# Splitting the squares of queries and keys: two fp32r products in place of one fp32 product

## The reference

```
def rmsnorm(x, g):
    xf = x.astype(jnp.float32)
    y = xf * lax.rsqrt(jnp.mean(xf * xf, axis=-1, keepdims=True) + EPS)
    return (y * g.astype(jnp.float32)).astype(x.dtype)
```

## Time and profile before

| | us |
|---|---|
| median of 3 runs | 3531.56 |
| lowest and highest | 3531.51, 3531.73 |
| profiled execution, its own time | 3533.1 |
| span of the profile (first to last instruction) | 3531.3 |
| attention layers, in the span | about 2340 to 3531 |
| TensorE's mean granted clock over the span | 0.985 of full |

### The profile page before, as it was taken

One profiled execution on the slowest core, in us unless ns is written; L12 is line 12 of the kernel. 1 busy time (PEld: TensorE's weight loads), 2 busy tenths in 40 slices (PEclk: granted clock), 3 DMA queues, 4 the chain that ended last, 5 costly groups with the idle time before them and its releaser, 6 DMA issues.

```text
span 3531.3 us, 45519 instructions
## 1 busy us (share of the span) xinstructions
PE 3380.8 (96%) x16418; PEld 2772.2 (79%) x16418; DVE 1505.3 (43%) x2496; ACT 1325.5 (38%) x2112; POOL 1414.2 (40%) x1040
## 2 busy tenths in 40 slices
PE   8999998899999999999979999979999999998898
PEld 7888876788888888887768888867777777887677
DVE  2221455552215522136565221472575377335633
ACT  3222435442224422233554222463344244444343
POOL 5554433045545455443304554343432433452222
PEclk9999999999999999999999999989999999999999
DMA  4322211022222232221202222322211221231111
GB/s 153 98 98 96 84 66 54 7 96 95 95 96 96 81 98 95 90 95 66 66 1 84 95 95 96 106 84 84 72 66 48 84 66 60 78 125 60 42 54 60
DMA packets 76660, 281.30 MB, mean 80 GB/s; under 512 B 8512, under 2 KB 8640, under 8 KB 76128
## 3 DMA queue, kind: packets, MB, share of 16 engines
q1 hardware_dynamic: 75600, 274.66, 23.6%
q10 hardware_dynamic: 912, 4.59, 0.4%
HBM read 277.12 MB, written 2.10 MB: 79 GB/s over the span
## 4 chain that ended last, share of the span: by engine, by line
PE 87%; DVE 7%; ACT 3%; issue 2%; DMA 1%; DVEq 0%; ACTq 0%; SPq 0%
PE ps L1795 16%; PE ps L1797 16%; PE ps L1796 16%; PE ps L1867 4%; PE ps L1869 4%; PE ps L1868 4%; PE ps L2316 2%; PE ps L2330 2%; PE ps L1906 2%; PE ps L1904 2%; PE ps L1905 2%; PE ps L2377 2%; PE ps L2257 1%; PE ps L2259 1%; PE ps L2258 1%
## 5 line engine op out<-in xcount | busy, mean ns | idle before, releaser
L545 POOL TENSOR_TENSOR w_lo<-raw,w_hi 128x512 fp32r<-128x512 f32 x1028 | 1402.6, 1387 | 2093.6 <-ACT w_hi L596 2093.5
L1795 PE MATMUL ps<-x_hi,w_hi 128*128 128x512 f32 x2560 | 1045.3, 408 | 4.6 <-issue 4.6
L1797 PE MATMUL ps<-x_hi,w_lo 128*128 128x512 f32 x2560 | 999.2, 390 | 0.0
L1796 PE MATMUL ps<-x_lo,w_hi 128*128 128x512 f32 x2560 | 998.6, 390 | 0.0
L596 ACT ACTIVATE w_hi<-raw 128x1024 fp32r<-128x1024 f32 x514 | 542.2, 1057 | 1099.0 <-PE ps L1797 617.7
L1795 PEld LDWEIGHTS ps<-x_hi,w_hi 128*128 128x128 f32 x2560 | 481.8, 188 | 125.1 <-issue 29.0
L1796 PEld LDWEIGHTS ps<-x_lo,w_hi 128*128 128x128 f32 x2560 | 481.7, 188 | 117.8 <-issue 22.1
L1797 PEld LDWEIGHTS ps<-x_hi,w_lo 128*128 128x128 f32 x2560 | 481.2, 188 | 102.6
L1224 DVE TENSOR_TENSOR T<-T,ps 128x512 f32<-128x512 f32 x66 | 45.3, 687 | 497.0 <-PE ps L1797 490.8
L1904 PE MATMUL ps<-h_hi,w_hi 128*128 128x512 f32 (+1 forms) x440 | 153.2, 348 | 0.0
L1906 PE MATMUL ps<-h_hi,w_lo 128*128 128x512 f32 (+1 forms) x440 | 152.5, 347 | 0.0
(11 more groups left out here) (330 smaller groups left out, 5088.8 us busy)
## 6 DMA issues: line engine op xcount, KB each, us to landing
raw<-in_weights SPq DMA_DIRECT2D x514, 512.0 KB, 3.3
Y<-in_x_t SPq DMA_DIRECT2D x1, 2048.0 KB, 7.9
mem<-in_mem_t ACTq DMA_DIRECT2D x2, 1024.0 KB, 7.2
out_t<-Y SPq DMA_DIRECT2D x8, 256.0 KB, 2.2
ple_p<-in_p_t ACTq DMA_DIRECT2D x2, 512.0 KB, 5.1
mat<-in_mats SPq DMA_DIRECT2D x1, 768.0 KB, 11.7
masks<-in_masks ACTq DMA_DIRECT2D x1, 768.0 KB, 8.4
rope<-in_rope_b ACTq DMA_DIRECT2D x1, 512.0 KB, 8.1
```

The source lines that it names most:

```text
L545: ins = pool.tensor_tensor(g.wl[:, k, part], g.raw[:, k, part], g.wh[:, k, part], ALU.subtract)
L1795: mm(out, wh[:, c], xh[:, kc, :], start=kc == 0, stop=False)
L1796: mm(out, wh[:, c], xl[:, kc, :], start=False, stop=False)
L1797: ins = mm(out, wl[:, c], xh[:, kc, :], start=False, stop=kc == DC - 1)
```

## The change

`g.T` slots 0 and 1, which were two buffers of squares, become one square (slot 0) and its high part (slot 1), under the name `g.SQ` in fp32r. ScalarE squares into slot 0, waits for that, and copies it to slot 1, which rounds to fp32r. POOL subtracts slot 1 from slot 0 in place (`square_low`). TensorE multiplies both parts by ones in fp32r into the same sum. The three tiles of `FAST` (r = 7, 31 and 65), whose sums are not inside a unit, keep the fp32 product. The memory keys, 256 columns wide, use the two halves of a slot in turn. On POOL, `square_low` of a unit u stands behind the low part of unit u+3 and ahead of that of unit u+4. A `Sum` inside a unit is issued ahead of chunk 6 and no longer ahead of chunk 4; groups stay ahead of chunk 4 and now come first in `mid`.

```diff
+        g.SQ, _ = place("square_parts", (P, 2, S), F32R, squares)
+        g.ones, _ = place("ones_r", (P, P), F32R)
@@ between
-            out.append(op._replace(mid=tuple(held) + ((op.mid,) if op.mid else ())))
+            out.append(op._replace(mid=((op.mid,) if op.mid else ()) + tuple(held)))
+FAST = (R_MEM[0] + 7, R_A + 23, R_B + 1)
+def parts(r):
+    return r + 1 - sum(f <= r for f in FAST)
+def square_cols(r, width):
+    return slice(r % 2 * N_MEM, r % 2 * N_MEM + N_MEM) if width == N_MEM else slice(0, width)
@@ pool_program
+    def square_low(r, width):
+        cols = square_cols(r, width)
+        pool.wait_ge(s.sqhi_done, parts(r))
+        pool.tensor_tensor(g.SQ[:, 0, cols], g.T[:, 0, cols], g.SQ[:, 1, cols], ALU.subtract).then_inc(s.sqlo_done, 1)
+    for i in range(2):
+        for r in range(2):
+            low_many(at, BASE["AB"][i] + (8, 6)[i])
+            at = BASE["AB"][i] + (8, 6)[i]
+            square_low(R_MEM[i] + r, N_MEM)
+        for op in PLANS[i]:
+            if isinstance(op, Unit) and op.r is not None and op.r not in FAST:
+                low_many(at, op.u + 4)
+                at = op.u + 4
+                square_low(op.r, N_MEM if op.kind == "mem_k" else S)
@@ norm (ScalarE, once)
+            fn(g.ones[:, :], g.mat[:, M_ONES, :], ACT.Copy).then_inc(s.ones_done, 1)
@@ qk_square
+        cols = square_cols(r, width)
         act.wait_ge(s.qraw_done, r + 1)
-        if r >= 2:
+        if width == S or r % 56 < 2:
+            if r >= 2:
+                act.wait_ge(s.qss_mm, r - (r % 56 == 1))
+        else:
             act.wait_ge(s.qss_mm, r - 1)
-        fn(g.T[:, r % 2, 0:width], src, ACT.Square).then_inc(s.qsq_done, 1)
+        fn(g.T[:, 0, cols], src, ACT.Square).then_inc(s.qsq_done, 1)
+        if r not in FAST:
+            act.wait_ge(s.qsq_done, r + 1)
+            fn(g.SQ[:, 1, cols], g.T[:, 0, cols], ACT.Copy).then_inc(s.sqhi_done, 1)
@@ tile
-            if kc == DC // 2:
-                for op in mid:
+            for op in mid:
+                if kc == (DC // 2 if isinstance(op, Group) else DC - 2):
                     item(op)
@@ item of a Sum
-            pe.wait_ge(s.qsq_done, r + 1)
+            cols, out = square_cols(r, width), ps[:, 2, 0:width]
             if r:
                 pe.wait_ge(s.qrs_done, r)
-            mm(ps[:, 2, 0:width], ones, g.T[:, r % 2, 0:width], start=True, stop=True).then_inc(s.qss_mm, 1)
+            if r in FAST:
+                pe.wait_ge(s.qsq_done, r + 1)
+                mm(out, ones, g.T[:, 0, cols], start=True, stop=True).then_inc(s.qss_mm, 1)
+            else:
+                pe.wait_ge(s.ones_done, 1)
+                pe.wait_ge(s.sqlo_done, parts(r))
+                mm(out, g.ones[:, :], g.SQ[:, 1, cols], start=True, stop=False)
+                mm(out, g.ones[:, :], g.SQ[:, 0, cols], start=False, stop=True).then_inc(s.qss_mm, 1)
```

More of the change, by code:

```diff
@@ L137, in build @@
         g.XL, _ = place("x_lo", (P, DC, S), F32R)
-        g.T, _ = place("T", (P, 7, S), F32)
+        g.T, squares = place("T", (P, 7, S), F32)
+        g.SQ, _ = place("square_parts", (P, 2, S), F32R, squares)
         g.vec, _ = place("vec", (P, N_VEC), F32)
@@ L209, in build @@
             e_done qdec_done ks_done r_done vn_mm vn_done o_mm o_copied ds_mm s_done osq_done oss_mm osr_done
-            memhi_done memlo_done qraw_done qsq_done qss_mm qrs_done qk_done vcopy_done
+            memhi_done memlo_done qraw_done qsq_done sqhi_done sqlo_done ones_done qss_mm qrs_done qk_done vcopy_done
             s_mm smax_done p_done pn_done pt_mm ptc_done o_mm2 o_done gate_done silu_g_done gout_done ohi_done olo_done proj_copied
```

## The result

| | before | after |
|---|---|---|
| median (4 runs each) | 3531.61 us | 3551.88 us |
| lowest and highest | 3531.51, 3531.73 | 3551.55, 3557.17 |
| ratio to before | | 1.0057, interval 1.0045 to 1.0069 |
| span of the profiled execution | 3531.3 | 3550.1 |

The change makes the kernel slower by 20 us. I predicted 3521, in a range up to 3534: the direction is wrong, and the time lies above the range.

A forecast was written before the change was run, and what follows sets the result against it. TensorE was taken to bound most cycles and VectorE some; -9.0 + 1.2 - 1.1 + 1.2 + 1.0 - 5.1 + 1.0 = -10.8 us, giving a median of 3520.8, predicted as 3521, range 3507 to 3534 (forecast's own 3512 to 3527).

The forecast's parts named there:

- The gain of the products: TensorE's sums: two fp32r products save 0.40 us per wide sum, 0.2 per narrow one, 27 us at most.
- POOL goes in front of L1601 and again in front of L1602, 0.98 each: VectorE's rotation: POOL's third instruction brings two blocks, making the chain 0.78 us longer in each of 48 units.
- The fourth rival: VectorE's chain: each block lasts POOL's whole 1.26 us, chain 1.34 longer a unit, +11, 3543; chance 5%.
- The lead of L1600 over POOL is then only 0.1; I take off 0.6: Six heads with groups: each gains 2.1 us, cut to 1.5 for where the lead is lost; -9.0 together.
- Rival 2: Lost race: in units without a group POOL starts before L1600, three blocks there; +5.5, 3537; chance 15%.
- Second half's first head, -1.1: Head without groups: of VectorE's 0.89 wait 0.78 goes, cycle 6.35 becomes about 6.15, six units at -0.19.
- First half's first head, +1.2: Head with a small group in each unit: VectorE's longer chain costs 0.2 us in each of six units.
- Behind the last heads, +1.0: Scores waiting for the last key's rotation: its sum comes 1.37 us later, less 0.4 for its earlier end.
- Memory, -5.1: Memory parts: seven wide and eight narrow sums -4.4, less 0.6 for short units, and -1.3 for matmuls moved ahead of a wait.
- Last layer, +1.0: One key -0.4, query units' saving absorbed by VectorE's chain, three sums now behind groups +1.4 together.
- the first rival: Full gain: POOL's extra instruction costs VectorE nothing that counts; -23, 3509; chance 22%.
- my own criterion: Wrong if a head still takes 51.4 us, or the new sums wait for POOL by more than 0.2 each.

The follow-up runs named there:

- e11: Changed kernel, sums ahead of groups inside units, subtraction in two pieces; in each half's later heads fp32 for tiles without following group, others at the middle: 3520.71 us.
- e3: Changed kernel with POOL's subtraction in two instructions of 256 columns in place of one of 512: 3529.26 us, ratio 0.9993.
- e7: As e6, but POOL's subtraction in one instruction of 512 columns: 3527.31 us, ratio 0.9985.
- e9: Changed kernel with one change of order: where a group lies inside the unit, the sum stands ahead of it at the middle: 3546.16 us, ratio 1.0039.
- e2: Changed kernel without POOL's subtraction, both products reading the high part (sum comes out doubled): 3519.98 us, ratio 0.9965.
- e6: Changed kernel, subtraction in two pieces, sums at the middle where a group follows and ahead of groups, fp32 for layer one's tiles without one: 3527.64 us.
- e1: Changed kernel with every sum in fp32 as before (no copy, no POOL subtraction), only the later place kept: 3545.65 us, ratio 1.0037.

## Why the prediction was wrong, by its steps

**The gain of the products: right, a little small.** I read 0.40 for a wide sum from starts. Where TensorE bounds the cycle, e11's is 9.22 (raw copies at 2577.61 and 2586.83) against 9.67 before (2578.96 and 2588.63): 0.45. With the two fp32r products at 0.46, an fp32 product of 512 columns costs 0.91 in the cycle, not 0.86. For a narrow sum give 0.29, of which I took 0.2 without a reason; eight of them make 0.7 us.

**"POOL goes in front of L1601 and again in front of L1602, 0.98 each": right, where no low part is under way.** Measured 1.65 to 1.67 twice, and a softmax multiply that ends 9.0 behind its raw copy (2590.01 to 2599.00), where I had worked out 9.01. A turn is shorter than POOL's instruction. The Trainium skill ("SBUF — State Buffer", section "Who interferes with whom") calls the port pair that VectorE and GpSimd share an exclusive lock, held for the whole instruction; it says the latter of VectorE's 2-port modes. The trace agrees on who waits for whom, and shows 0.98 for one of 1.26 (512 columns) and 0.42 in e3 (256). The fourth rival would have given 3543 by that rule, nearer than my number, but with L1638 at 1.94, which no row shows.

**"The lead of L1600 over POOL is then only 0.1; I take off 0.6": this is the step that failed.** I saw the narrow margin (it measured 0.23) and priced it as an accident. It is lost in every unit behind one without a group, twice a head: the third instruction on POOL keeps POOL busy longer (1.60 + 3.43 where the earlier trace rows have 2.99), and its tail holds up the next unit's normalising by 0.32, more than the 0.23 by which L1637 leads in the unit before. e7 has no third instruction in that unit and wins the race. I had followed POOL's queue forward to the weights (spare by three units) and not forward to VectorE's next instruction. The cost for a head, by the distance of starts: two waits for the softmax multiply of 1.4 each, with 0.06 more for the transposes behind each (0.71 to the next product, not 0.65), and two of 0.3 where the sum itself waits for POOL in the unit without a group. That last was my 0.1. POOL is done when I said, 3.98 behind the raw copy (I had 4.0), but TensorE's next product starts 0.46 and the one behind it 0.31 after the one before, where 0.23 is usual. With six sums at -0.45 this is +0.9, and the raw copies say +0.94 (2572.61 to 2624.03 before, 2573.45 to 2625.81 after). Predicted: -1.5. Rival 2 had the lost race and its size for a group (1.2), with a head at +0.2, but another place and trigger. It put the race in the units without a group and had POOL start early, less than 2.15 behind the raw copy. Here POOL starts at 2.38, as I had it, and it is VectorE that is late. The first groups of each half, where VectorE is behind already, cost 3.1 us in the first half (raw copies 2555.70 to 2572.61 of before) and 2.0 in the second (2840.84 to 2857.74), and not 0.6.

**Second half's first head, -1.1: failed with it.** From the third unit on each has three blocks, and from the fourth on the sum waits 1.1 for POOL as well: cycle 7.2, as rival 2 had it (raw copies at 2819.08 and 2826.30 of after). From the fourth on rival 2's trigger holds too: POOL starts 2.08 behind the raw copy. It came to +3.3.

**First half's first head, +1.2: too dear.** +0.2. Three units take 0.15 to 0.42 more, and the others give that back.

**Behind the last heads, +1.0: wrong in sign but small** (-0.6, with the granted clock in it).

**Memory, -5.1: -3.2.** Up to the last memory query after stands at -4.06, e9, with the same code up to there, at -2.64: 1.4 us of such a number is not the kernel's. Then 1.7 is lost again behind it; see the clock below.

**Last layer, +1.0: failed, an omission.** I counted the sum's move behind the group as 0.46 on TensorE, and did not ask who waits for its result. ScalarE's root and VectorE's chain stand behind it, and VectorE's chain bounds this layer. Measured +8.3, of which 6.3 go with the order (e9), some 3 by the chain and the rest by the granted clock.

Of the 29.6 us between -10.8 and +18.8, the heads are 18.6, the last layer 7.3, the second first head 4.4. POOL's new instruction costs 32 us (e2) against the 27 that I gave to the products; the distance from the first rival to the forecast (3509 to 3521) had put it at 12.

Of what I said would show it: L1602 (now L1639) at 1.67 and L1600 at 0.68 holds in four of the six units of a head, L1600 at 1.7 as well in the two behind a unit with no group. A head takes 52.4, so by my own criterion the prediction was wrong. (The 49.3 that I gave there leaves out my own 0.6; with it, it is 49.9.)

## What to carry to other kernels

When work is added to an engine that is idle for more than half of the time, follow its queue until it is empty again, and lay that against every neighbour it can hold up, the next iteration's first instruction too. A margin that is smaller than the delay which the change itself adds is lost each time and not now and then. Split a new side instruction into pieces if its neighbours only need to get past it (22 us between after and e3, but hardly anything between e7 and e6, where the tight units had none), and give the new form of the product only to the tiles that have the time for it: e11 keeps fp32 in two tiles of six in most heads, and is the only complete version whose gain is, with its whole interval, 0.2% or more.

## What the runs showed that I had not expected

**The order on POOL protects VectorE.** With two pieces of 256 columns, TENSOR_TENSOR on VectorE takes 1.10 and 1.11 in place of 1.67 and 1.67, and the third block, the one of the lost race, vanishes, though POOL's own work is longer (2.19 for 1.28 in that unit, and for 1.60 in the one before it). The time went from 3551.88 to 3529.26.

**The clock after the same wait is not the same.** Behind the memory queries TensorE idles by the same amount in before, after, e1, e9 and e11 (16.7 to 16.8 busy of 20). Windows 2410 to 2430 of before, after, and e1:

```profile
2410.00:2430.00 20.00, 16.79 (x70) 1.00 0.17 53
```

```profile
2410.00:2430.00 20.00, 16.70 (x65) 0.91 0.24 78
```

```profile
2410.00:2430.00 20.00, 16.70 (x58) 0.83 0.16 53
```

1.00 in before and in e9, 0.91 in after and e11, 0.83 in e1, and the next raw copy loses up to 2.7 us against before (1.7 in after, 2.7 in e1, 0.1 in e9). The wait is there in all. After and e9 run the same code up to there and still differ, so the code ahead does not decide it alone; what does, no run shows. How far a kernel is ahead of before at that point does not sort them either: e9 (2.6) has 1.00, e3 (2.9) and after (4.1) have 0.91, e2 (5.1) has 1.00 again. It limits what a sum of terms can predict here to a few us.
